# Latent attention's scores in two rotary passes instead of three, with the mask in one of them

## The reference

```python
sc = jnp.einsum('bqhd,bkhd->bhqk', qn_i, k_nope) + jnp.einsum('bqhr,bkr->bhqk', qr_i, k_rope)
sc = sc.astype(jnp.float32) * scale
q_chunk = (i * Q_BLOCK + jnp.arange(Q_BLOCK)) // CHUNK
mask = k_chunk[None, :] <= q_chunk[:, None]
sc = jnp.where(mask[None, None], sc, -jnp.inf)
p = jax.nn.softmax(sc, axis=-1).astype(v.dtype)
```

## Time and profile before

| what | us |
|---|---|
| median of three runs | 1964.98 (1963.58 to 1965.52) |
| the profiled execution, span from first to last instruction | 1962.9 |
| TensorE busy in it | 1940.2 |
| the latent stage's heads, 510 to 625 us of the span | 115 |

### The profile page before, as it was taken

How to read it: one execution, slowest core, us unless ns; L and a number is a source line. 1 busy time by engine, 2 the same in 40 slices (tenths; PEclk the granted TensorE clock), 3 DMA queues, 4 the chain that set the end, 5 groups by cost and what they waited for, 6 DMA issues and landing times.

```text
span 1962.9 us, 27288 instructions
## 1 busy us (share of the span) xinstructions
PE 1940.2 (99%) x10578; PEld 1675.1 (85%) x10578; DVE 1248.2 (64%) x2219; ACT 827.2 (42%) x1377; POOL 319.8 (16%) x257
## 2 busy tenths in 40 slices
PE   9999999999999999999999999999999999999997
PEld 8998888888888988898888889887888888888897
DVE  7676666267775754388777525786673877774256
ACT  5233333244565532344444334465554444442343
POOL 2332332101241100201111010120112011110102
PEclk9999999999999999999999999999999999999998
DMA  5323222222212235322232322232112222233221
GB/s 173 104 76 100 87 81 91 92 86 94 69 44 76 78 99 137 108 90 93 86 107 98 119 88 84 83 122 78 44 55 86 87 86 96 98 109 117 96 66 64
DMA packets 54839, 179.02 MB, mean 91 GB/s; under 512 B 6167, under 2 KB 10775, under 8 KB 54712
## 3 DMA queue, kind: packets, MB, share of 16 engines
q1 hardware_dynamic: 54712, 177.29, 28.8%
HBM read 172.55 MB, written 4.72 MB: 90 GB/s over the span
## 4 chain that ended last, share of the span: by engine, by line
PE 93%; DVE 4%; ACT 1%; issue 1%; POOL 0%; DMA 0%; SPq 0%; DVEq 0%; ACTq 0%; POOLq 0%
PE pb L829 88%; PE pb L2737 1%; PE pb L932 1%; DVE WL L810 1%; PE pb L916 1%; DVE FR L1048 0%; PE pb L1767 0%; PE pb L2782 0%; DVE X L1013 0%; PE pb L920 0%; PE pb L1414 0%; DVE FR L903 0%; ACT WH L799 0%; DVE FD L1004 0%; DVE T L3011 0%
## 5 line engine op out<-in xcount | busy, mean ns | idle before, releaser
L829 PE MATMUL pb<-FR,WH 128*128 128x512 f32 (+1 forms) x5100 | 1443.2, 369 | 6.2 <-DVE FR L1048 3.2
L829 PEld LDWEIGHTS pb<-FR,WH 128*128 128x128 f32 x5100 | 914.5, 189 | 163.5 <-issue 5.9
L829 PE MATMUL pb<-FR,WL 128*128 128x512 f32 (+1 forms) x2550 | 934.9, 367 | 0.0
L810 DVE TENSOR_TENSOR WL<-stage,WH 128x1024 fp32r<-128x1024 f32 (+1 forms) x311 | 401.5, 1308 | 403.2 <-ACT WH L799 402.1
L829 PEld LDWEIGHTS pb<-FR,WL 128*128 128x128 f32 x2550 | 480.7, 189 | 79.6
L799 ACT ACTIVATE WH<-stage 128x1024 fp32r<-128x1024 f32 (+1 forms) x311 | 319.8, 1051 | 115.1 <-PE pb L829 108.6
L829 PE MATMUL pb<-WH,FR 128*128 128x256 f32 x832 | 155.9, 285 | 0.4 <-DVE WL L810 0.4
L829 PEld LDWEIGHTS pb<-WH,FR 128*128 128x128 f32 x832 | 131.6, 192 | 1.2 <-DVE WL L810 0.8
L1291 POOL TENSOR_TENSOR acc<-acc,T 128x512 f32<-128x512 f32 (+1 forms) x52 | 64.1, 1233 | 408.8 <-ACT T L1262 273.9
L829 PEld LDWEIGHTS pb<-FR 128*128 128x128 f32 x752 | 109.3, 190 | 10.8 <-issue 2.6
L829 PE MATMUL pb<-WL,FR 128*128 128x256 f32 x416 | 117.7, 283 | 0.0
(11 more groups left out here) (237 smaller groups left out, 1654.2 us busy)
## 6 DMA issues: line engine op xcount, KB each, us to landing
stage<-in_ws SPq DMA_DIRECT2D x310, 512.0 KB, 3.6
scr<-FD SPq DMA_DIRECT2D x16, 160.0 KB
X<-in_xT SPq DMA_DIRECT2D x8, 256.0 KB, 6.4
FD<-in_decay SPq DMA_DIRECT2D x8, 256.0 KB, 3.9
FD<-scr SPq DMA_DIRECT2D x1, 2048.0 KB, 8.5
out_dram<-X SPq DMA_DIRECT2D x16, 128.0 KB, 1.7
FD<-in_rope_b SPq DMA_DIRECT2D x2, 512.0 KB, 3.6
FD<-in_pT SPq DMA_DIRECT2D x4, 256.0 KB, 4.9
```

The source lines that it names most:

```text
L810: dve.tensor_tensor(lo, src, hi.bitcast(F32), ALU.subtract).then_inc(*self.tick("w_lo", ("w_lo", u)))
L829: m = pe.matmul(out, l, r, start=first and i == 0, stop=last and i == n - 1)
```

## The change

Heads are no longer interleaved by 32 rows: the rotary tile holds one head in its first 64 rows and the other in its last 64. Two stationary tiles are made per head: qa has the head's hi in its own 64 rows and the rest in the other 64; qb has the hi in its own rows and mask constants in the other 64. The moving tiles are ka, the key's hi in both halves, and kb, the key's rest in the head's own rows and mask constants in the others. Then qa ka is hi hi + lo hi, and qb kb is hi lo + mask: a group of five matmuls. Turning by halves of 32 rows takes four B products instead of two, in `dve_rope`, for the shared key and for each of the four pairs. The hi of a pair is made in four ScalarE copies of 64 rows (two per head), and the rest by two VectorE subtractions of 64 rows (`rotary_rest`) in place of one GpSimd subtraction of 128. ScalarE makes the odd head's copies (`rope_odd`) in the odd head before, behind divide 2. The mask comes in two loads of 128x512 and five GpSimd copies; ScalarE's two mask copies go, as does one of its two copies for the shared key. Slots of the loop's temporaries are fixed instead of taken in turn.

```diff
-ROPE_KV = tuple(256 + i % 32 + 32 * (i // 64) for i in range(128))
+ROPE_KV = tuple(256 + i % 64 for i in range(128))
 def rope_q(h):
-    return tuple(192 * (h + i // 32 % 2) + 128 + 32 * (i // 64) + i % 32 for i in range(128))
+    return tuple(192 * (h + i // 64) + 128 + i % 64 for i in range(128))
...
-        seat(tmp.next(), "t", "lat", "mask")
+        for i in range(2):
+            seat(tmp.next(), "t", "lat", "mask", i)
...
-        tm = Ring(self.tmps[4:6] + [Slot(self.R)])
+        own = {"A": self.tmps[4], "B": self.tmps[5], "q": self.tmps[5], "pv": self.tmps[4], "k": Slot(self.R)}
...
-    def dve_rope(self, dve, t, key, bank, tab, tabw):
+    def dve_rope(self, dve, t, key, bank, tab, tabw, half):
...
-        dve.tensor_tensor(B[64:128, :], b[0:64, :], Sn[0:64, :], ALU.mult)
-        dve.tensor_tensor(B[0:64, :], b[64:128, :], Sn[64:128, :], ALU.mult).then_inc(
-            *self.tick("rope_mul", ("rope_mul", t, *key), ("free", *bank)))
+        for o in range(0, P, 2 * half):
+            dve.tensor_tensor(B[o + half:o + 2 * half, :], b[o:o + half, :], Sn[o:o + half, :], ALU.mult)
+            m = dve.tensor_tensor(B[o:o + half, :], b[o + half:o + 2 * half, :], Sn[o + half:o + 2 * half, :], ALU.mult)
+        m.then_inc(*self.tick("rope_mul", ("rope_mul", t, *key), ("free", *bank)))
...
     def pe_lat(self, pe):
...
-                for w in (("q", h), ("k", h), ("qr", h // 2), ("kr", 1), ("mask",)):
+                for w in (("q", h), ("k", h), ("qa", h), ("qb", h), ("kr",), ("mask",)):
...
-            self.mm(pe, b[:, 0:n], [(rh, th), (rh, tl), (rl, th), (qh, kh), (qh, kl)], True, False)
-            self.mm(pe, b[:, n - 128:n], [(self.MK[:, 0:128], self.MK[:, 128:256])], False, False)
-            self.mm(pe, b[:, 0:n], [(ql, kh)], False, True).then_inc(*self.tick("pe_scores", ("pe", "lat", "s", h, i)))
+            self.mm(pe, b[:, 0:n], [(qb, kb), (qa, ka), (qh, kh), (qh, kl), (ql, kh)]).then_inc(
+                *self.tick("pe_scores", ("pe", "lat", "s", h, i)))
...
     def act_lat(self, act):
...
+            rotated(self.lat_qa, h, "qa_hi")
+            rotated(self.lat_qb, h, "qb")
+
+        def rope_odd(h):
+            rotated(self.lat_qb, h, "qb")
+            rotated(self.lat_qa, h, "qa_hi")
+
+        def rotated(slots, h, what):
+            own, _ = self.lat_own(h)
+            before = h - (4 if h % 2 else 2)
+            act.wait_ge(*(self.at("pe", "lat", "s", before, 3) if before >= 0 else self.at("mask")))
+            act.activation(self.lat_rot(slots, h)[own, :], self.place["t", "lat", "A", h - h % 2][own, :],
+                           ACT.Copy).then_inc(*self.tick("rotary_hi", (what, h)))
...
                 rope(0)
                 query(0)
+                rope_odd(1)
...
+            divide(h, 0)
             if after and not even:
                 rope(h + 1)
-            divide(h, 0)
...
             divide(h, 2)
+            if after and not even:
+                rope_odd(h + 2)
             scores(h, 3)
...
     def dve_lat(self, dve):
...
+        def rotary_rest(h):
+            own, other = self.lat_own(h)
+            a, q = ("t", "lat", "A", h - h % 2), self.lat_rot(self.lat_qa, h)
+            dve.wait_ge(*self.at("qa_hi", h))
+            dve.tensor_tensor(q[other, :], self.place[a][own, :], q[own, :].bitcast(F32), ALU.subtract).then_inc(
+                *self.tick("rotary_lo", ("qa", h), *([("free", *a)] if h % 2 else [])))
...
                 query(0)
+                rotary_rest(0)
+                rotary_rest(1)
...
                 query(h + 1)
+            if after and not even:
+                rotary_rest(h + 1)
             invert(h, 2)
             scores(h, 3)
+            if after and not even:
+                rotary_rest(h + 2)
             if h:
                 values(h - 1)
...
     def pool_lat(self, pool):
...
-            q, A = self.lat_qr[h // 2 % 2], ("t", "lat", "A", h)
-            pool.wait_ge(*self.at("qr_hi", h // 2))
-            pool.tensor_tensor(q[:, 512:1024], self.place[A], q[:, 0:512].bitcast(F32), ALU.subtract).then_inc(
-                *self.tick("qr_lo", ("qr", h // 2), ("free", *A)))
...
+        pool.wait_ge(*self.at("mask_in"))
+        for i, slots in enumerate((self.lat_qb, self.lat_kb)):
+            t = ("t", "lat", "mask", i)
+            for slot in slots:
+                pool.tensor_copy(slot, self.place[t]).then_inc(*self.tick("mask", ("mask",), ("free", *t)))
         add("kv", 1, ("t", "lat", "kvsq", 1))
```

More of the change, by code:

```diff
@@ L563, in rope @@
             for x in "AB":
-                seat(tm.next(), "t", "lat", x, h)
+                seat(own[x], "t", "lat", x, h)
         def head(what, h):
             seat(pr.next(), "lat", what, h)
-            seat(tm.next(), "t", "lat", what, h)
+            seat(own[what], "t", "lat", what, h)
         def value(h):
@@ L582, in values @@
             seat(bank[7], "lat", "pv", h)
-            seat(tm.next(), "t", "lat", "pv", h)
+            seat(own["pv"], "t", "lat", "pv", h)
         for h in range(8):
@@ L1526, in qk_out @@
             bank = ("ret", "qk", h, n) if h else ("ret", "w", n)
-            self.dve_rope(dve, "ret", (h, n), bank, self.ret_tab, ("tables", "ret"))
+            self.dve_rope(dve, "ret", (h, n), bank, self.ret_tab, ("tables", "ret"), 64)
         def gate(h, e, later=False):
@@ L1935, in act_lat @@
         self.hi_to(act, BLOCK["w_in_b", KD - 1, 3])
-        for par in range(2):
-            act.wait_ge(*self.at("rope", "lat", "kr"))
-            act.activation(self.lat_kr[:, 1024 * par:1024 * par + 512], self.place["t", "lat", "A", "kr"], ACT.Copy,
-                           scale=self.masks[:, par:par + 1]).then_inc(*self.tick("lat_hi", ("lat_hi", "kr", par)))
+        act.wait_ge(*self.at("rope", "lat", "kr"))
+        act.activation(self.lat_ka, self.place["t", "lat", "A", "kr"], ACT.Copy).then_inc(
+            *self.tick("lat_hi", ("lat_hi", "kr")))
         self.hi_to(act, BLOCK["w_in_b", KD - 1, 4])
@@ L2219, in sp_lat @@
         self.load_to(sp, BLOCK[WIDE["lat"][-1][0], KD - 1, WIDE["lat"][-1][1]])
-        for w in self.freed("t", "lat", "mask"):
-            sp.wait_ge(*w)
-        sp.dma_start(self.place["t", "lat", "mask"][:, 0:128], self.ins["mask"][:, :]).then_inc(
-            *self.tick("mask_in", ("mask_in",), by=16))
-        sp.wait_ge(*self.at("kr", 1))
+        for i in range(2):
+            for w in self.freed("t", "lat", "mask", i):
+                sp.wait_ge(*w)
+            sp.dma_start(self.place["t", "lat", "mask", i], self.ins["mask"][:, 512 * i:512 * i + 512]).then_inc(
+                *self.tick("mask_in", ("mask_in",), by=16))
+        sp.wait_ge(*self.at("kr"))
         tables(1)
@@ L3399, in shape_constants @@
         c, s = np.cos(a)[i], np.sin(a)[i]
-        s = np.where(np.arange(128)[:, None] < 64, s, -s)
+        s = np.where(np.arange(128)[:, None] // half % 2 == 0, s, -s)
         out[name] = np.concatenate([c, s], axis=1).astype(f)
     out["ident"] = np.eye(128, dtype=f)
-    qq, kk = np.arange(128)[:, None], np.arange(128)[None, :]
-    out["mask"] = np.where(kk // 64 <= qq // 64, 0.0, NEG).astype(f)
-    par = (np.arange(128) // 32) % 2
-    out["masks"] = np.stack([par == 0, par == 1], axis=1).astype(f)
+    at, row = np.arange(512)[None, :], np.arange(128)[:, None] % 64
+    own, early = at // 128 == row, at % 128 < 64
+    out["mask"] = np.concatenate([np.where(own & early, 1.0, 0.0), np.where(own & ~early, NEG, 0.0)], axis=1).astype(f)
     dist = 511 - np.arange(TW)
```

63 lines of the change are left out of this document (28 added, 35 removed).

## The result

| | before | changed |
|---|---|---|
| median of 4 runs each | 1964.88 us (1963.58 to 1965.52) | 1981.20 us (1979.45 to 1982.08) |
| span of the profiled execution | 1962.9 us | 1977.5 us |
| mean granted clock of TensorE | 0.997 | 0.994 |

The ratio is 1.0081, with a 95% interval from 1.0069 to 1.0093: slower by 16.3 us. The forecast was 1977.0, in a range of 1969 to 1982. The profiled execution took 1979.45 us and is the quickest of the four; the others lie up to 2.6 us above it.

A forecast was written before the change was run, and what follows sets the result against it. Bound: TensorE and an equally full loop of VectorE and ScalarE. Sum: 2.3 + 3.8 - 0.8 + 3.8 + 3.4 = 12.5, less 0.6 in head 7, +11.9 us; 1964.98 + 12 = 1977.0, range 1969 to 1982.

The forecast's parts named there:

- TensorE is full, and another loop is just as full: Heads' stretch: VectorE and ScalarE, from one rope to the next, form a loop as long as TensorE's work.
- Rival (a): Whole kernel: TensorE is the only bound, all added work lies beside it; -8.6 us, 1956.4; chance 0.08.
- Entry and before head 0: Ahead of the loop: TensorE stands 1.0 us, key(1) starts 3.4 late; head 0 returns 1.07, leaving 2.3 us late.
- The odd head's loop: Heads 1, 3, 5: added VectorE and ScalarE work delays divide 3, +3.8 us, in head 5 taken as 3.4.
- From rope to rope: Heads' stretch: even heads return no delay, so lateness adds up from 2.3 to 12.5 us at head 7's first output tile.
- the spare at rope(4): At rope(4) the bank was free 0.87 us early, expected to absorb 0.8 us of the delay.
- One expected sign: TensorE would wait 1 to 2 us for the value rests at every rope and at head 7's output.
- Rival (b): Even heads: the loop takes up delay there, so each odd head costs 2.3 us; +8.2, 1973.2; chance 0.17.
- Head 7: Last head, without rope: blocks 2 and 3 are bound by TensorE and give back 0.6 us.
- The mask copies: Entry: five GpSimd copies of the mask lie in idle time, 0 to 1.4 us; taken as 0 in the sum.
- rival (d): Entry: the first rests stand behind all five mask copies; +13.3 us, 1978.3; chance 0.12.
- (c): Rope products and copies: low instructions cost half price; +3.3 us, 1968.3; chance 0.05.

The follow-up runs named there:

- w1: Kernel before, without the product of the queries' rotary rest and the mask matmul, nothing else changed: 1962.52 us against 1964.60, ratio 0.9990.
- x2: Changed kernel with a sixth matmul (query's rest times key's rest) in each block of scores: 1979.80 us, 1.0075 of the kernel before.
- x1: Kernel before with only rope's two 64-row products cut into four of 32 rows: 1971.40 us, +5.6 against before.
- x3: Changed kernel with the second head's two copies and rest moved from the odd head into the following even head: 1973.07 us, +7.2 against before.
- y2: x3 with the first head's rest moved from in front of inverse 2 to behind inverse 3: 1971.34 us, +6.8 against before.
- z1: Stacked hi and rest with the 32-row interleaving kept, one query tile a head, rests of heads 2, 4, 6 on GpSimd: 1963.78 us, 0.9997 of before.

## Why the prediction was right, and where it was off

**The bound.** "TensorE is full, and another loop is just as full" holds: w1 won 2.1 of 8.6 us, and of the 5.2 that x2 added 1.6 were left behind head 7, 1.1 of them expected in heads 0 and 7. Rival (a), 1956.4, is out.

**Entry and before head 0.** Expected: TensorE stands 1.0 us at the gate, key(1) 3.4 late, rope(2) 2.3 late. Measured: 1.00; 513.29 - 510.00 = 3.29; 528.31 - 526.03 = 2.28. The stretch went as laid out; since the changed kernel's profile is 0.3 us ahead at 450 us, the cost is that much more. The rope products of heads 2 and 6, before and changed:

```profile
526.03 0.69 DVE L1310 TENSOR_TENSOR R<-pb,FD 128x512 f32<-128x512 f32 x1
...
579.11 0.69 DVE L1310 TENSOR_TENSOR T<-pb,FD 128x512 f32<-128x512 f32 x1
```

```profile
528.31 0.69 DVE L1311 TENSOR_TENSOR T<-pb,FD 128x512 f32<-128x512 f32 x1
...
589.07 0.69 DVE L1311 TENSOR_TENSOR T<-pb,FD 128x512 f32<-128x512 f32 x1
```

**The odd head's loop.** Expected +3.8, measured 14.26 - 10.10 = 4.16 in head 3 (14.26 in head 1 too). The order of the waits was right, and the sizes drifted by tenths. Counted from rope's start, expected and measured: divide 2 9.88 and 9.93, exponential 3 11.48 and 11.74 (the two copies take 1.17, not 1.10, and exponential 3 starts behind their end, not 0.1 before it), the gated values 12.24 and 12.58, divide 3 13.88 and 14.26. x1, x3 and y2 price the pieces: products 1.3 a pair, the second head's copies and rest 1.73, the first head's rest 0.93. Together 3.9 to 4.0.

**From rope to rope.** Expected lateness 2.3, 5.3, 9.1 and, at the tile, 12.5; measured 2.28, 5.81, 9.96 and 13.72. Heads 1 and 3 cost 3.53 and 4.15, where 3.0 and 3.8 were expected; of the spare at rope(4) 0.6 came back, not 0.8. Head 5 cost 3.76, not 3.4: the 0.4 by which VectorE waited for TensorE there came back, but from the 4.15 that a loop costs (head 3), not from 3.8. One expected sign did not show: TensorE was to wait 1 to 2 us for the value rests at every rope and at head 7's output, and it waits 0.76 at rope(2), 0.32 at rope(4), not at all at rope(6), 0.50 at head 7's. It loses its time at divides 2 and 3 instead; in x3, which takes the stand at divide 3 away, the ones at the value rests grow to 1.46 and 2.25. Rival (b), that even heads take up the delay, is out: 8.2 at most.

**Head 7.** Expected -0.6. Measured 13.07 - 13.72 = -0.65, by the transposes of block 3 there, before and changed:

```profile
620.52 0.60 PE L1767 MATMUL pb<-ident,T 128*128 128x128 f32 x4
```

```profile
633.59 0.60 PE L1780 MATMUL pb<-ident,T 128*128 128x128 f32 x4
```

**The mask copies.** Five in 2.85 us from 456.45, over at 459.3, and the key's rests that wait for them start at 470.19:

```profile
456.45 2.85 POOL L2222 CAST FR<-T 128x512 fp32r<-128x512 f32 x5 [51.44 <-DMA T<-in_mask]
```

Zero was right and rival (d) is out. Half-height work at half price (c) is out as well: 0.68 to 0.69 for 32 rows on VectorE, 0.58 for a ScalarE copy of 64.

**What the sum lacked.** The step that failed is the end of the sum: 12.5 - 0.6 was carried unchanged to the end of the span. The heads cost 13.07, the two profiled spans differ by 14.6, the medians by 16.3. The 1.5 us between the first two arise at one place: VectorE's instructions start 13.04 us later than in the kernel before at 1271 us of its span and 14.54 later at 1292, and in the second profile of the changed kernel 16.79 and 18.29. There the granted clock fell, 0.83 for the 10 us from 1280 in the first profile. The change does not touch that stretch, and the kernel before, 13 us earlier, is at 1.00 there, with the same stands of TensorE (0.51 and 0.35 us, against 0.51 and 0.34) and 8.48 us busy of 10:

```profile
1267.00:1277.00 10.00, 8.48 (x68) 7.88 (x67) 8.47 (x25) 4.09 (x8) 0.73 (x1) 1.00 0.34 107
```

The other 1.7 us lie between the first profiled execution and the median. The second profile, of a slower execution, has 2.9 more at rope(2), behind the stand at key(1), and 0.9 more from rope(2) to rope(4), both behind falls of the clock; which of this the executions without a profile had is not known. The prediction named that stand (2.4 us there, 1.0 at the entry) and priced it as time only. Why the clock falls at 1280 stays open: it fell there in both profiles of the changed kernel and in none of the twelve others, and no run was made for it.

**How much of it was luck.** The median lies 0.8 us inside the upper end of the range. The delay in the heads, which the prediction worked out as 11.9, is 13.1 of the 16.3 us; the rest fell into a margin that was set without a reason from a row ("as much again for pauses I did not count").

## What to carry to other kernels

An engine's busy share says little about what a saving wins; take the work out alone first, as w1 does, and see what reaches the end. Where two engines hand one piece to and fro, each instruction put between hand-overs counts in full, whatever its height, and a place that the timeline shows idle may be idle because GpSimd's work makes it useless for a VectorE subtraction. A stand of TensorE of over 2 us cost its length here and, about every second time, half speed behind it; that second part cost from nothing (behind head 3's block 3) to 2.9 us (behind key(1), where TensorE bounds what follows).

## What was not expected of the hardware

- In the heads' stretch the granted clock fell to half behind stands of 2.0 to 2.8 us, but not behind each: 13 times behind 26 such stands in the fourteen profiles. At key(1) it fell in one of two profiles of the same kernel, and behind block 3's transposes in two of three places in the first of them and in all three in the second. Behind the stands of 1.65 us or less there it never fell. At 1280 it fell with no stand over 0.51 us ahead.
- A GpSimd subtraction of 32x512 took as long as one of 128x512, 1.29 us (the median of six in z1, up to 1.49); a GpSimd copy of 128x512 with rounding took 0.62, 0.57 apart.
- Two VectorE subtractions of 32x512 took 1.38 us alone and 2.36 beside a GpSimd subtraction.
